# Condition products of a two-block network moved from VectorE to GpSimd, with a third weight buffer in the feed-forward stages

## The reference

```python
def first_block(x, c, w_ada, b_ada, ...):
    cond = jax.nn.silu(c)
    for l in range(DEPTH):
        mod = (cond @ w_ada[l] + b_ada[l]).astype(x.dtype)[:, None, :]
        sh1, sc1, g1, sh2, sc2, g2 = jnp.split(mod, N_MOD, axis=-1)
        h = _rmsnorm(x, norm1_w[l]) * (1.0 + sc1) + sh1
        x = x + g1 * _token_mixers(h, w_in[l], ..., w_out[l])
        h = _rmsnorm(x, norm2_w[l]) * (1.0 + sc2) + sh2
        x = x + g2 * _conv_ffn(h, w_up[l], conv_f_w[l], w_down[l])
    return _rmsnorm(x, final_norm_w)

def _conv_ffn(h, w_up, conv_w, w_down):
    u = _depthwise_conv(h @ w_up, conv_w)
    gate, val = jnp.split(u, 2, axis=-1)
    return (jax.nn.gelu(gate, approximate=False) * val) @ w_down
```

## Time and profile before

| what | value |
|---|---|
| median of three runs | 3004.89 us |
| profiled execution | 3002.57 us |
| span of its program | 3000.8 us |
| granted clock, mean | 0.957 |
| PE busy | 2800.5 us (93%) |
| PEld busy | 2160.0 us (72%) |
| DVE busy | 1758.3 us (59%) |
| ACT busy | 1125.0 us (37%) |
| POOL busy | 212.5 us (7%) |
| DMA | 289.25 MB, mean 96 GB/s |

### The profile page before, as it was taken

The page is one execution under the profiler, slowest core; times in us unless marked ns, Lnnn a source line. Parts: engine busy times, 40 slices in busy tenths (PEclk is TensorE's granted clock), DMA queues, the critical chain, the costliest instruction groups (busy, mean ns, idle before and its releaser), DMA issues.

```text
span 3000.8 us, 36584 instructions
## 1 busy us (share of the span) xinstructions
PE 2800.5 (93%) x14716; PEld 2160.0 (72%) x14716; DVE 1758.3 (59%) x3323; ACT 1125.0 (37%) x1875; POOL 212.5 (7%) x178
## 2 busy tenths in 40 slices
PE   3999889999999988899998999989998999999998
PEld 2966667778877766778886878656676878666676
DVE  6767948887464785787446467634425247634424
ACT  3253344333334334333223552244313462243312
POOL 0000000110000000011000231000110131000110
PEclk7999799999999978999999999989999999999999
DMA  7441114555332111355223332121223212121222
GB/s 228 146 125 57 55 57 140 171 194 171 96 90 64 55 55 43 126 174 177 96 87 112 117 113 92 56 64 43 78 77 99 75 43 72 56 85 43 71 72 83
DMA packets 301464, 289.25 MB, mean 96 GB/s; under 512 B 7152, under 2 KB 298096, under 8 KB 301296
## 3 DMA queue, kind: packets, MB, share of 16 engines
q1 hardware_dynamic: 299008, 278.84, 29.3%
q0 software_dynamic: 960, 5.51, 0.6%
q10 hardware_dynamic: 1328, 2.57, 0.2%
HBM read 284.80 MB, written 2.10 MB: 96 GB/s over the span
## 4 chain that ended last, share of the span: by engine, by line
PE 79%; DVE 13%; ACT 5%; issue 2%; DMA 1%; DVEq 0%; POOL 0%; ACTq 0%; POOLq 0%
PE ps L502 78%; DVE adaacc L1240 3%; PE ps L671 2%; DVE wl L1234 2%; DVE ug L1240 1%; DVE ca L1240 1%; ACT ug L835 1%; DVE hl L1240 1%; DVE recat L1448 1%; DMA xT<-in_xT 0%; ACT rr L835 0%; DVE rawt L1240 0%; DVE uv L1240 0%; DVE s L1487 0%; ACT s L835 0%
## 5 line engine op out<-in xcount | busy, mean ns | idle before, releaser
L502 PE MATMUL ps<-hh,wh 128*128 128x512 f32 x2288 | 940.4, 411 | 61.2 <-DVE wl L1234 30.6
L502 PE MATMUL ps<-hh,wl 128*128 128x512 f32 x2288 | 901.6, 394 | 0.0
L502 PE MATMUL ps<-hl,wh 128*128 128x512 f32 x2288 | 901.6, 394 | 0.0
L1234 DVE TENSOR_TENSOR wl<-raw,wh 128x2048 fp32r<-128x2048 f32 (+2 forms) x186 | 411.3, 2212 | 342.0 <-ACT wh L835 341.6
L502 PEld LDWEIGHTS ps<-hh,wh 128*128 128x128 f32 x2288 | 434.2, 190 | 204.7 <-issue 78.5
L502 PEld LDWEIGHTS ps<-hh,wl 128*128 128x128 f32 x2288 | 434.6, 190 | 96.3
L502 PEld LDWEIGHTS ps<-hl,wh 128*128 128x128 f32 x2288 | 435.6, 190 | 89.0 <-issue 7.0
L835 ACT ACTIVATE wh<-raw 128x2048 fp32r<-128x2048 f32 (+2 forms) x186 | 342.8, 1843 | 257.4 <-PE ps L502 129.4
L1240 DVE SCALAR_TENSOR_TENSOR adaacc<-raw,cond,adaacc 128x256 f32<-128x256 f32 x448 | 223.7, 499 | 16.0
L835 ACT ACTIVATE rawt<-ps 128x512 f32<-128x512 f32 (+1 forms) x106 | 63.3, 597 | 348.3 <-PE ps L502 348.2
L502 PEld LDWEIGHTS ps<-recq,reck 64*128 64x128 f32 x1728 | 126.5, 216 | 48.7 <-issue 32.8
(11 more groups left out here) (226 smaller groups left out, 3540.7 us busy)
## 6 DMA issues: line engine op xcount, KB each, us to landing
raw<-in_w_in SPq DMA_DIRECT2D x74, 1024.0 KB, 5.3
raw<-in_w_ada SPq DMA_DIRECT2D x64, 1024.0 KB, 5.3
raw<-in_w_up SPq DMA_DIRECT2D x44, 1024.0 KB, 6.2
raw<-in_w_in SPq DMA_DIRECT2D x44, 512.0 KB, 5.3
raw<-in_w_out SPq DMA_DIRECT2D x16, 1024.0 KB, 5.3
raw<-in_w_down SPq DMA_DIRECT2D x16, 1024.0 KB, 5.5
stage<-in_w_ada SPq DMA_DIRECT2D x8, 1024.0 KB, 12.4
raw<-in_w_down SPq DMA_DIRECT2D x8, 768.0 KB, 4.4
```

Source lines behind the costliest of these rows:

```text
L502: return e.matmul(o, a, b, start=start, stop=stop, skip_group_check=True)
L1234: return e.tensor_tensor(o, a, b, op)
```

## The change

The chunks of the first block, and those for the second block's first layer, which are summed during the first block and its last feed-forward stage, are made on POOL (`adap`): one product of the whole chunk with the condition, in place in the raw buffer, then halves added three times, the last into `adaacc`. The 12 chunks of the second block's second layer stay on DVE. The chunks stand behind every second weight instead of every one; of the 20 chunks of layer 1 that stood in layer 0's feed-forward stage, the 8 that the start of layer 1's mixer needs stay there and 12 move into that mixer. By stage the chunks on the plan are 12, 24, 0, 16 and 12 before (mixer 0, feed-forward 0, mixer 1, feed-forward 1, second block), and 12, 12, 12, 16 and 12 after. In the feed-forward stages the loads use three raw buffers, each the one used longest ago; the third lies in the memory that the mixers use for other things, so its first load waits for the last attention step. The gelus get a unit of their own (`ge`), behind the split of the next weight.

```diff
@@ Memory
         self.uv = [sb(f"uv{i}", [128, 512]) for i in range(3)]
+        self.raw.append(sb(f"raw{NR}", [128, 2048]))
@@ COST
-    ... "ada": (("DVE", 4.0, True),),
+    ... "ada": (("DVE", 4.0, True),), "adap": (("POOL", 10.0, True),),
@@ Order.split_one
-            self.run(("ada", j))
+            self.run(("ada" if self.plan[j]["key"][0] == 2 and self.plan[j]["key"][1] == 1 else "adap", j))
@@ scalar_program
             conv3_centre(("ug", l, ch), ...)
-            go.wait_ge(*at("conv3", ("ug", l, ch)))
-            act(M.ug[s][:, :], M.ug[s][:, :], ACT.Gelu).then_inc(*up("act_gelu", ("gelu", l, ch)))
+
+    def gelu(l, ch):
+        s = ch % 4
+        go.wait_ge(*at("conv3", ("ug", l, ch)))
+        act(M.ug[s][:, :], M.ug[s][:, :], ACT.Gelu).then_inc(*up("act_gelu", ("gelu", l, ch)))
@@ gpsimd_program
+    def ada(j):
+        p = plan[j]
+        acc, v = M.adaacc[X.acc[p["chunk"]]], M.piece(M.raw[p["slot"]], p, 0)
+        c0 = 0 if p["chunk"][0] == 1 else 8
+        go.wait_ge(*at("raw", j))
+        go.wait_ge(*at("small", "cond"))
+        weights = M.cond[:, c0:c0 + KD].rearrange("p (k n) -> p k n", n=1).broadcast_to([128, KD, 256])
+        e.tensor_tensor(v, v, weights, ALU.mult).then_inc(*up("pool_ada"))
+        for k in (4, 2):
+            go.wait_ge(*last("pool_ada"))
+            e.tensor_tensor(v[:, 0:k, :], v[:, 0:k, :], v[:, k:2 * k, :], ALU.add).then_inc(*up("pool_ada"))
+        go.wait_ge(*last("pool_ada"))
+        if X.acc_before[p["chunk"]] is not None:
+            go.wait_ge(*at("sums", X.acc_before[p["chunk"]]))
+        e.tensor_tensor(acc[:, :], v[:, 0, :], v[:, 1, :], ALU.add).then_inc(*up("pool_ada", ("acc", p["chunk"])))
@@ sync_program
-        if j >= NR:
-            freed = {"two": "wl", "raw": "w_used", "ada": "raw_summed"}[plan[j - NR]["kind"]]
-            go.wait_ge(*(at("acc", plan[j - NR]["chunk"]) if freed == "raw_summed" else at(freed, j - NR)))
+        if p["raw_before"] is not None:
+            before = plan[p["raw_before"]]
+            go.wait_ge(*(at("acc", before["chunk"]) if before["kind"] == "ada" else
+                         at("wl" if before["kind"] == "two" else "w_used", p["raw_before"])))
+        if p["after_attention"] is not None:
+            go.wait_ge(*at("s3", "1", p["after_attention"], 2, 3))
@@ prepared
-        p["slot"] = j % NR
+        p["slot"] = i = min(range(NR + 1 if long_ else NR), key=lambda i: -1 if raw_in[i] is None else raw_in[i])
+        p["raw_before"], raw_in[i] = raw_in[i], j
@@ order_ffn, up
             j = o.use(("upv", l, ch))
+            for x in range(2):
+                o.put("ge", l, ch + x)
@@ make_plan, strew
-            i = min(i + 1, len(plan))
+            i = min(i + step, len(plan))
@@ make_plan
-    block1(0)
-    strew(ada(1, 0, (2, 4, 3)), 0)
-    at = len(plan)
-    ffn(0)
-    strew(ada(1, 0, (5,)) + ada(1, 1, (1, 0, 2, 4, 3)), at)
-    block1(1)
...
+    for weights, extra, step in ((lambda: block1(0), ada(1, 0, (2, 4, 3)), 2), (lambda: ffn(0), ada(1, 0, (5,)) + ada(1, 1, (1, 0)), 2),
+                                 (lambda: block1(1), ada(1, 1, (2, 4, 3)), 2), (lambda: ffn(1), ada(1, 1, (5,)) + ada(2, 0, (1, 0, 2)), 2),
+                                 (lambda: block2(0), ada(2, 1, (1, 0, 2)), 1), (lambda: block2(1), [], 0)):
+        at = len(plan)
+        weights()
+        strew(extra, at, step)
```

More of the change, by code:

```diff
@@ L229 @@
 COST = {
-    "part": (("PE", 1.38, True),), "split": (("ACT", 1.9, True), ("DVE", 2.3, True)), "ada": (("DVE", 4.0, True),),
+    "part": (("PE", 1.38, True),), "split": (("ACT", 1.9, True), ("DVE", 2.3, True)), "ada": (("DVE", 4.0, True),), "adap": (("POOL", 10.0, True),),
     "adasum": (("PE", 0.25, True), ("DVE", 0.2, True)),
@@ L1652, in gpsimd_program @@
 def gpsimd_program(e, X):
-    M, up, at, last, go = X.M, X.tally.up, X.tally.at, X.tally.last, Go(e)
+    M, up, at, last, go, plan = X.M, X.tally.up, X.tally.at, X.tally.last, Go(e), X.plan
     def loaded():
@@ L1697, in branch @@
             e.tensor_tensor(M.merged[:, o, :], M.merged[:, o, :], raw[:, :], ALU.add).then_inc(*up("pool_merge", ("merged", l, nm, o)))
[L1699 removed]
+    parts = {"loaded": loaded, "adap": ada, "gb": bias, "uv": up_value, "rope": rope, "ch": c_low, "tm": index_mask, "br": branch}
     for who in ("sv", "c0"):
@@ L1736, in prepared @@
     splits = 0
+    raw_in, layer, long_ = [None] * (NR + 1), None, False
     for j, p in enumerate(plan):
-        p["slot"] = j % NR
+        if p["kind"] != "ada":
+            was, long_ = long_, p["key"][0] in ("upg", "upv", "down")
+            layer = p["key"][1] if long_ and not was else layer
+        p["long"] = long_
+        p["slot"] = i = min(range(NR + 1 if long_ else NR), key=lambda i: -1 if raw_in[i] is None else raw_in[i])
+        p["raw_before"], raw_in[i] = raw_in[i], j
+        p["after_attention"] = layer if i == NR and (p["raw_before"] is None or plan[p["raw_before"]]["after_attention"] != layer) else None
         off, p["views"], p["loads"], p["srcs"] = 0, [], [], [src for _, _, src in p["pieces"]]
@@ L2052, in ada, with strew @@
         return [((which, l, j), (w, l, 0, KD, 256 * j, 256)) for m in ms for j in range(4 * m, 4 * m + 4)]
-    def strew(extra, first):
+    def strew(extra, first, step):
         i = first
         for key, piece in extra:
-            i = min(i + 1, len(plan))
+            i = min(i + step, len(plan))
             plan.insert(i, {"kind": "ada", "key": key, "pieces": [src(*piece)], "join": False})
             i += 1
-        return plan
     def block1(l):
```

10 lines of the change are left out of this document (1 added, 9 removed).

## The result

The changed kernel takes 3090.17 us (median of four runs, 3089.65 to 3091.77) beside 3005.47 us for the kernel before: a ratio of 1.028, 95% interval 1.026 to 1.030. It is 85 us slower. The forecast was slower, but by 13 us, and its range ended at 3044 us. The profiled execution has a span of 3090.0 us against 3000.8.

The account below looks back on a forecast made before the run. PE's own work was taken to bound the kernel, DVE in the mixer tails and a few handovers. Terms -3 + 20 - 15 - 8 + 21 and 0.7 gave +16 us on 3002.6: 3018 us, range 2974 to 3044.

Parts of the forecast that it names:

- the price of DVE's time: In the mixers, each us taken from DVE was put at 0.42 us of span, from comparing the two layers.
- X: Span that POOL's chunks cost each mixer by keeping DVE out: 17 us, with ends 0 and 30 us.
- part 2: 52 chunks come onto POOL, which holds DVE 5 us a chunk in the mixers: 17 us in each layer.
- part 1: 52 chunks leave DVE: layer 0's mixer 20 us less, layer 1's mixer about 3 us more for eight added sums.
- part 3: Feed-forward stages, steady: three buffers and one chunk to two weights save 15 us in layer 0, 8 us in layer 1.
- part 4: Start of each feed-forward stage: three chunks behind the last output weight come late on POOL, +10.5 us, twice.
- raw buffers at nothing: In the mixers, a chunk holding one of two raw buffers through load and POOL work was costed at nothing.
- gelu move 0: In the feed-forward stages, gelus behind the next split remove an ACT wait that nobody waited for: worth nothing.
- the third buffer ends the chain of 11 us: In feed-forward, weights sharing one raw buffer took about 11 us each; three buffers and fewer chunks remove that chain.
- POOL disturbs more: Rival: holds in the recurrence idle PE and halve the clock, 30 us in both layers; +42, 3044 us; chance 0.08.
- little disturbance: Rival: DVE gets in between a long POOL instruction's pieces, about 4 us a mixer; -21, 2982 us; chance 0.34.
- The third buffer does nothing: Rival: feed-forward pairs stay at 23.8 us, only the 12 sums are saved there; +35, 3037 us; chance 0.04.

Follow-up runs that it names:

- little on DVE: The kernel before with third buffer and gelu units, seven of eight operations of every DVE chunk cut to 16 of 256 columns: 2973.6 us.
- little on POOL: The changed kernel with POOL's four operations of a chunk cut to 16 of 256 columns: 2981.5 us.
- all on DVE: The changed kernel with all 64 chunks on DVE again; new order, third buffer and gelu units stay: 2998.9 us, ratio 0.998 to the kernel before.
- POOL in ffn: The changed kernel with POOL for the chunks of the feed-forward stages alone, those of the mixers on DVE: 3014.0 us.
- the run with the third buffer and the gelus: The kernel before with only the third buffer and gelu units added; old plan, all chunks on DVE: 2989.3 us, ratio 0.995.

## Why the prediction was wrong

The direction was right; the size was not. The step that failed is the price of DVE's time, 0.42 us of span per us, put on time that POOL holds back: it gave X = 17 us in each mixer, and X came to 41.5 and 36.3 us.

My own sum was +16 us and the profiled span grew by 89. Of the 73 us between them the two Xs of part 2 are 44, part 1 is 10, part 3 is 9, part 4 is 9 and the rest of the program 1. By its steps:

- **Part 1, chunks leave DVE (-20 and +3 us in the mixers).** Without POOL's hold the mixers change by 321.1 - 335.9 = -14.8 and 327.2 - 319.1 = +8.1 us. The price of 0.42 us of span per us of DVE is the step that failed: "little on DVE" gives 0.14, and "little on POOL" against "all on DVE" 4.1 us for 25.5 us in the first front, 0.16. With the clock alike it is less still: 0.04 as above, and 1.9 us for 25.4 us, 0.08, against "POOL in ffn", whose front is that of "all on DVE" at the clock of 0.99 that "little on POOL" has:

```profile
66.82:316.57 249.75, 243.10 (x1714) 193.02 (x1714) 176.08 (x379) 105.10 (x179) 2.13 (x4) 0.99 0.34 106
```

The 0.42 came from comparing the two layers' mixers, 338 against 312 us. Cut at the same instruction they are 335.9 and 319.1 us: 9 of my 26 us were the edges of my windows, since I began the second stage at 854 us and its first matmul stands at 846.9. Of the -14.8, 10.0 us are there with all chunks on DVE too (12.9 us in "POOL in ffn"): they come with the new order, which leaves four chunks behind the mixer, and the output projection pays 10.3 us for that.
- **Part 2, the hold (X = 17 us a layer, at most 30).** Its mechanism was right and its amount on DVE too: I took 5 us a chunk, 40 us for eight, and DVE is busy 36.1 + 7.1 us (front and tail) and 31.1 + 10.3 us more. Again the price failed. X came to 362.6 - 321.1 = 41.5 and 363.43 - 327.16 = 36.3 us. I had priced held DVE time as DVE's own work, but a chunk on DVE is eight instructions of 0.5 us, while a hold of 3.6 us falls on whatever is next, `recq` and `reck` on PE's chain among it, and the granted clock falls with it (0.93 and 0.94 in place of 0.99 and 0.97 in the fronts). The runs show 0.8 to 1.0 us of span per us in place of 0.42, and 0.2 to 0.45 where POOL's instructions were short. That price is the step that cost most: the two Xs are 78 us in place of 34.
- **The rule of the Trainium skill in part 2** (GPSIMD Engine Reference, "Key points"), by which `TENSOR_SCALAR` would be held as well, would have added 2 us to X. In the changed kernel `att_s` stayed at 484 ns (483 before): no `TENSOR_SCALAR` of its mixers ran while POOL was at work. But the rule shows in the run with the third buffer and the gelus, where the chunk's first operation on DVE, 0.34 us alone, meets POOL's gating product:

```profile
552.68 1.32 DVE L1241 TENSOR_SCALAR adaacc<-raw,cond 128x256 f32<-128x256 f32 x1
552.25 1.61 POOL L1671 TENSOR_TENSOR ug<-ug,uv 128x512 f32<-128x512 f32 x1 [1.10 <-DVE uv L1244]
```

- **Part 2, raw buffers at nothing.** This held: between 66 and 330 us ACT's splits waited 1.8 us for loads in the changed kernel, against 13.4 us before, and in the second mixer's front not at all in either. The second mixer's +8.1 us without the hold has other parts: eight sums, a sum that waits 1.3 us, and 3.8 us at one `wl` in the new order, which I had not foreseen; I did not take them apart further.
- **Part 3, feed-forward (-15 and -8 us).** Without the hold -16.4 and -6.7 us, nearly my numbers, for the wrong reason in the main: "gelu move 0" and "the third buffer ends the chain of 11 us" are both wrong, and the errors cancel. The chain of loads in the earlier trace rows was there, but the load was not what came last; ACT's queue was. That two errors cancelled is luck; the pairs came to 22.3 us, as I had said. The hold then took back 4.5 and 5.0 us. `fl` had time, as I had it: it is longer (0.93 us on average in the first stage, 0.68 with little on POOL), but PE never waits for it. PE waits 1.5 us for `hl` and 1.3 us for one `wl` in the first stage, whose begin is at half clock for 9.6 us instead of 5.4, and 3.9 us for three `wl` in the second.
- **Part 4, the starts (+10.5 us each).** Measured +13.4 and +17.6, inside the bounds of 0 to 18. The cause was the one I named, the row of three chunks, but it acted by SP's queue and DVE's queue behind `wl`, not by the shift's sum. With the chunks on DVE the same order costs +10.3 us by another wait: there PE stands 5.1 us, once in each output projection, until DVE has made a chunk whose sum stands next in PE's order.
- **The rivals.** "POOL disturbs more" named the recurrence, the planner that knows nothing of the hold, and the clock, all of which came; its X of 30 was still too small, and a chance of 8 in 100 was too low for it. The evidence I held for little disturbance, that PE is full in a mixer's first half, was true of a kernel without holds and says nothing of what a hold of 3.6 us does. "The third buffer does nothing", at 4 in 100, was true of the buffer: alone it left the pairs at 23.8 us. The changed kernel got its shorter pairs from the gelus' place, which I had put at nothing, and from the thinner spreading.

## What to carry to other kernels

Work is not free because an engine is idle: ask what its instructions lock, for how long one at a time, and who waits for the engine that is locked out. The price of delay is not the price of work; a long single delay on an engine that feeds PE costs nearly its full length here, the clock behind it included, while the same time in pieces under a us is absorbed by half or more (0.45 and 0.2 us of span per us here, against 1.0 and 0.8). And where a wait is named after one engine, look at what stood in that engine's queue, and in the queue ahead of it, before giving the wait to a buffer; an edit that looks like tidying (the gelus) was the only part of this change that is shown to make the kernel faster.

## What the runs showed of the hardware that was not expected

- POOL's product of 128x2048, one input a broadcast, takes 3.60 us when nothing meets it, under the 4.4 us scaled from the earlier trace rows; its mean in the changed kernel, 4.33 us, holds DVE's share of the hold.
- The hold works both ways: POOL's last addition had a mean of 1833 ns beside a busy DVE and 0.74 us alone.
- On POOL the one-input piece of 256 columns was the slower one: 1.10 us on average against 0.82 us with two tensors. It is so without a hold too: the shortest of 416 took 0.91 us, against 0.60 us.
- Idle times of PE at the recurrence were followed by stretches at the lower of its two clocks, 1.2 GHz. Two such places in the first mixer of the changed kernel, idle times of 5.49 us (to 223.40) and 4.48 us (to 245.96), each as the window that holds most of the idle time and the one behind it:

```profile
217.00:222.00 5.00, 0.91 (x4) 0.39 (x3) 5.00 (x4) 0.00 (x0) 4.77 (x4) 0.95 0.03 11
222.00:228.00 6.00, 4.60 (x22) 3.63 (x22) 4.33 (x13) 2.57 (x6) 0.63 (x1) 0.50 0.63 175
241.00:246.00 5.00, 0.52 (x7) 0.31 (x5) 5.00 (x6) 2.37 (x3) 4.63 (x4) 0.94 0.00 0
246.00:252.00 6.00, 6.00 (x34) 4.84 (x36) 3.41 (x13) 0.60 (x1) 0.00 (x0) 0.50 0.00 1
```

PE stands still while POOL and DVE are busy, and the granted clock is 0.50 behind it. In the first mixer's front the hold makes PE idle for 21 us more and, at the lower clock, busy for 15 us more.
